# First block's merge-gate and branch projections with tokens on the partitions, and block sums in its down stage for three of eleven pairs

## The chip, the cores and the metric

One core of one Trainium2 chip. The metric is the device time in microseconds of one execution. The kernel before takes 1254.74 us (median of 3 runs, 1254.57 to 1254.82). The core's engines run side by side, each in its own order: TensorE (PE; its weight loads are shown as PEld), VectorE (DVE), ScalarE (ACT), GpSimd (POOL), and SyncE (SP), which issues the loads. They wait for one another by semaphores.

## The reference, cut to what matters

Two transformer blocks on x of 256 tokens by 1024, fp32. The first block's part around the change:

```python
h = rms_norm(x, norm_mix_w)
proj = h @ w_in            # q, kv, gates, q_ret, k_ret, v_ret, g_ret, g_merge (2 * 1024)
y_a = nsa_attention(...) @ w_nsa_branch            # 512 -> 1024
o_r = head_group_norm(retention(...)) * silu(g_ret)
y_b = o_r @ w_ret_branch                           # 1024 -> 1024
gate_a, gate_b = split(sigmoid(g_merge), 2)
x = x + (gate_a * y_a + gate_b * y_b) @ w_mix_out
h = rms_norm(x, norm_ffn_w)
u = causal_dwconv(h @ w_ffn_up)                    # 1024 -> 2 * 2816, width 3
x = x + (silu(u_gate) * u_val) @ w_ffn_down        # 2816 -> 1024
```

The second block has two layers with attention, a convolution and a Fourier branch, a gated merge and the same kind of feed-forward; the change leaves its arithmetic alone.

## The kernel before, in words

**Products.** Every fp32 product is three matmuls with operands split into an upper and a lower part: upper by upper, upper by lower, lower by upper (`mul3`). There are two forms. In `rows` the tokens are stationary (128 of them, half `tt`) and 512 weight columns move (lines 529 to 531): the result has tokens on the partitions. In `feats` 128 weight columns are stationary and all 256 tokens move (lines 584 to 586): the result has features on the partitions. The up stage of the feed-forward has its own form, `wide_feats` (line 608, upper and lower parts of the tokens side by side as 512 columns, then line 613, 256 columns).

**Weights.** `PLAN` lists chunks of 128x2048 (1 MB) in the order of use; `UNITS` names the chunks of each projection. SP loads chunk i into one of six raw buffers when chunk i - 6 has been used (line 436). ACT makes the upper part `whi` (line 1235, four buffers). The lower part `wlo` overwrites the raw chunk; DVE makes it (line 1955), or POOL in four quarters (line 1785) for the chunks in `POOL_LO`, among them three of every four units of the first block's up stage (`POOL_UP`). `splits(last)` makes the parts up to a chunk of the plan; ACT and DVE call it with a chunk three ahead of PE (AHEAD = 3).

**Order.** Each engine's program is written out by hand in the same order of units. `weave(front, back, n)` takes a step of `front` (the attention's small products) and then n steps of `back` (projections that don't depend on it), and runs the rest of `back` at the end. In the first block the back of the attention is vr0, vr1, sg0, sg1 (rows) and three of the eight merge-gate units gm0 to gm7 (feats); the other five stand behind retention. Then follow ya0, ya1 (feats), the transposes of the retention's result, yb0 to yb3 (feats), mo0 and mo1 (`to_x`), the norm n1, the up stage up0_0 to up0_21 and the down stage dn0. The gm units are scaled per token while they leave the banks; as tokens lie along the free axis there, the scale is turned first: two DVE copies (line 2162), two PE transposes (line 703), an ACT copy, and a wait of SP for it (line 133) before it loads tables into the place the scratch had. The merged product is `mg`, features on the partitions, which is what mo needs as stationary operand.

**Up stage.** For unit f ACT copies a bank (`us`, line 1570), makes `whi` of a later chunk, the silu (`fs`), the upper part `ghi` of an earlier product (line 1283) and the convolution's bias term (`fu`, line 1561). DVE does the convolution (line 2469), the product `fg` (line 2492) and the scaling (lines 2479, 2483). POOL makes its weight splits and the lower part `glo` of unit f - 6 (line 1816). `fg` has four buffers.

**Down stage.** Eleven pairs of `g` chunks, 24 matmuls of 512 columns each, into four banks (token half by column half). In the second block's two layers the pairs `SEVEN` = (1, 3, 5, 7), counted from 0, use block sums in the manner of Strassen and Winograd: seven products of blocks in place of eight, 21 matmuls in place of 24. They need a further chunk of sums of weight blocks (`weight_sums`, DVE, lines 1933, 1937, 1939, from the raw chunk, then split like any other), sums of the product's blocks (`g_sums`, POOL, lines 1885 and 1896, with ACT's upper part in between), and at the end `sevens_added` on DVE (line 2533), which adds the kept products to x. The last two or three chunks are ordered so that the first token half ends early: its x add (line 2428) and norm run beside the second half, and PE turns the normed half (line 548).

## Time and profile before

| | |
|---|---|
| median of 3 runs | 1254.74 us (1254.57 to 1254.82) |
| profiled execution | 1254.49 us |
| its span | 1253.2 us |
| instructions | 19361 |
| PE busy | 1247.4 us (100%), 7794 matmuls |
| DVE, ACT, POOL busy | 951.5 (76%), 714.7 (57%), 437.3 us (35%) |
| granted TensorE clock | full in all slices |
| chain that ended last | PE 96% |

A line of the page or of the trace gives an engine, the line of the kernel, the operation, the output and inputs, the shape and the count. Busy time is what the engine executes; a matmul's duration overlaps the next, so the price of a matmul is read from one start to the next. Idle time stands in brackets with what ended it.

### The profile page before, as it was taken

What the parts mean: (1) busy time and instruction counts of PE and PEld (TensorE: products, weight loads), DVE (VectorE), ACT (ScalarE), POOL (GpSimd) and SP (SyncE); (2) the same over time, 40 slices, a digit from 0 to 9 for tenths busy, and PEclk for the clock granted to TensorE, in tenths of its full rate; (3) what the DMA queues carried; (4) which work ended last, traced back from release to release, by engine and by line L of the source; (5) the groups of instructions that cost most, each with busy time, mean ns of one, the idle gap of its engine ahead of it and who ended that gap; (6) DMA issues with size and microseconds to landing.
All of it is one profiled execution on the core that took longest, in us unless ns stands there. A gap on an engine that the chain in (4) does not pass through costs nothing.

```text
span 1253.2 us, 19361 instructions
## 1 busy us (share of the span) xinstructions
PE 1247.4 (100%) x7794; PEld 1120.3 (89%) x7794; DVE 951.5 (76%) x1372; ACT 714.7 (57%) x1026; POOL 437.3 (35%) x346
## 2 busy tenths in 40 slices
PE   9999999999999999999999999999999999999999
PEld 7888899988888889899998888888999998888887
DVE  6865677767887378985767888986898586888895
ACT  7755445377665365575836555545456674655552
POOL 0010011039992069467450112008756743011100
PEclk9999999999999999999999999999999999999999
DMA  7853334545455447644455554555853444545442
GB/s 303 310 211 135 124 129 141 196 185 202 174 197 199 170 168 237 220 164 136 168 191 185 182 200 145 190 210 189 271 188 144 158 168 168 191 181 200 151 166 121
DMA packets 36568, 230.77 MB, mean 184 GB/s; under 512 B 4480, under 2 KB 5120, under 8 KB 10496
## 3 DMA queue, kind: packets, MB, share of 16 engines
q1 hardware_dynamic: 36480, 229.55, 50.9%
q8 instruction: 61, 1.00, 0.3%
q14 instruction: 27, 0.22, 0.1%
HBM read 222.19 MB, written 1.05 MB: 178 GB/s over the span
## 4 chain that ended last, share of the span: by engine, by line
PE 96%; DVE 1%; DMA 1%; ACT 0%; issue 0%; SPq 0%; DVEq 0%
PE ps L608 19%; PE ps L529 10%; PE ps L531 10%; PE ps L530 10%; PE ps L613 10%; PE ps L584 9%; PE ps L585 9%; PE ps L586 9%; PE ps L534 6%; PE ps L548 2%; DMA raw<-in_w 1%; PE ps L677 1%; PE ps L1150 1%; DVE wlo L1955 1%; PE ps L845 0%
## 5 line engine op out<-in xcount | busy, mean ns | idle before, releaser
L1235 ACT ACTIVATE whi<-raw 128x2048 fp32r<-128x2048 f32 (+1 forms) x213 | 401.8, 1891 | 112.6 <-PE ps L531 66.9
L1955 DVE TENSOR_TENSOR wlo<-raw,whi 128x2048 fp32r<-128x2048 f32 (+2 forms) x169 | 383.7, 2276 | 89.0 <-ACT whi L1235 88.0
L1785 POOL TENSOR_TENSOR wlo<-raw,whi 128x512 fp32r<-128x512 f32 x176 | 227.2, 1324 | 90.5 <-ACT whi L1235 87.5
L608 PE MATMUL ps<-hh,whi 128*128 128x512 f32 x1056 | 255.8, 392 | 0.0
L608 PEld LDWEIGHTS ps<-hh,whi 128*128 128x128 f32 x1056 | 193.0, 188 | 36.5
L584 PE MATMUL ps<-hh,whi 128*128 128x256 f32 x640 | 184.1, 288 | 0.0
L586 PE MATMUL ps<-hh,wlo 128*128 128x256 f32 x640 | 181.0, 283 | 0.0
L585 PE MATMUL ps<-hh,whi 128*128 128x256 f32 x640 | 180.9, 283 | 0.0
L1757 POOL TENSOR_TENSOR st<-st,sm 128x1 f32<-128x1 f32 (+2 forms) x28 | 44.8, 1599 | 365.1 <-DVE st L2019 195.1
L613 PEld LDWEIGHTS ps<-hh,wlo 128*128 128x128 f32 x1056 | 137.8, 191 | 6.7
L613 PE MATMUL ps<-hh,wlo 128*128 128x256 f32 x1056 | 139.8, 282 | 0.0
L584 PEld LDWEIGHTS ps<-hh,whi 128*128 128x128 f32 x640 | 122.5, 191 | 0.4 <-issue 0.2
L585 PEld LDWEIGHTS ps<-hh,whi 128*128 128x128 f32 x640 | 122.5, 191 | 0.4 <-issue 0.2
L586 PEld LDWEIGHTS ps<-hh,wlo 128*128 128x128 f32 x640 | 122.4, 191 | 0.0
L2612 DVE SCALAR_TENSOR_TENSOR ps<-gp,sm,ps 128x256 f32<-128x256 f32 x232 | 99.3, 482 | 0.0
L529 PE MATMUL ps<-whi,hh 128*128 128x512 f32 (+1 forms) x248 | 97.9, 395 | 0.0
L531 PE MATMUL ps<-whi,hh 128*128 128x512 f32 (+1 forms) x248 | 95.3, 384 | 0.0
L530 PE MATMUL ps<-wlo,hh 128*128 128x512 f32 (+1 forms) x248 | 95.1, 383 | 0.0
L529 PE MATMUL ps<-whi,ghi 128*128 128x512 f32 x224 | 87.4, 390 | 0.0
L530 PE MATMUL ps<-wlo,ghi 128*128 128x512 f32 x224 | 87.2, 389 | 0.0
L531 PE MATMUL ps<-whi,glo 128*128 128x512 f32 x224 | 87.2, 389 | 0.0
L1570 ACT ACTIVATE fu<-ps 128x512 f32<-128x512 f32 x44 | 26.4, 599 | 101.5 <-PE ps L613 101.5
(350 smaller groups left out, 2266.2 us busy)
## 6 DMA issues: line engine op xcount, KB each, us to landing
raw<-in_w SPq DMA_DIRECT2D x203, 1024.0 KB, 4.8
raw<-in_w SPq DMA_DIRECT2D x8, 256.0 KB, 6.8
kst<-kh SPq DMA_DIRECT2D x16, 128.0 KB, 3.0
qst<-qh SPq DMA_DIRECT2D x16, 128.0 KB, 2.4
raw<-in_w SPq DMA_DIRECT2D x2, 560.0 KB, 12.9
x<-in_x SPq DMA_DIRECT2D x2, 512.0 KB, 5.3
gain<-in_rows SPq DMA_DIRECT2D x2, 512.0 KB, 7.8
kst<-kl SPq DMA_DIRECT2D x8, 128.0 KB, 2.7
```

The costliest lines, as they stand in the source:

```text
L529: pe.op.matmul(o, sh, mh, start=start, stop=False, skip_group_check=True)
L530: pe.op.matmul(o, sh, ml, start=False, stop=False, skip_group_check=True)
L531: signalled(pe.op.matmul(o, sl, mh, start=False, stop=stop, skip_group_check=True), names)
L584: pe.op.matmul(o, wh[:, k, c:c + 128], hi[:, k, :], start=first, stop=False, skip_group_check=True)
L585: pe.op.matmul(o, wh[:, k, c:c + 128], lo[:, k, :], start=False, stop=False, skip_group_check=True)
L586: ins = pe.op.matmul(o, wl[:, k, c:c + 128], hi[:, k, :], start=False, stop=last, skip_group_check=True)
L608: pe.op.matmul(o[:, :], wh[:, k, c], t.hh[:, k, :, :], start=k == 0, stop=False, skip_group_check=True)
L613: ins = pe.op.matmul(o[:, 0:S], wl[:, k, c], t.hhi[:, k, :], start=False, stop=k == 7, skip_group_check=True)
L1235: act.op.activation(t.whi[i % NHI][:, c], t.raw[i % NRAW][:, c], ACT.Copy).then_inc(*at("act_hi", ("hi", i)))
L1785: pool.op.tensor_tensor(t.wlo[i % NRAW][:, half(k)], t.raw[i % NRAW][:, half(k)], t.whi[i % NHI][:, half(k)].bitcast(F32), ALU.subtract).t ...
L1955: dve.op.tensor_tensor(t.wlo[i % NRAW][:, c], t.raw[i % NRAW][:, c], t.whi[i % NHI][:, c].bitcast(F32), ALU.subtract).then_inc(*at("dve_lo ...
L2612: ins = dve.op.scalar_tensor_tensor(t.cv[:, f, :] if j == 30 else acc, t.gp[:, f, j:j + S], cw[:, f, j:j + 1], acc, ALU.mult, ALU.add)
```

## The change

Part A: the merge gates are four units of 512 columns with tokens on the partitions (`rows`) in place of eight with features there; ACT and DVE scale one token half each on the way out of the banks. ya is done by a new form `short_rows`, yb by `rows`. The transposed scale and all that made it are gone. The merged product has tokens on the partitions now and is turned by 16 PE transposes (`mixed_turned`), the first half of the columns inside yb1, the second inside mo. `weave` no longer runs the back out, and the count of back steps behind each front step is given by `behind` and the yields. The x sum of mo takes its chunks in another order. Part B: the plan's down stage is made by one function for all three layers, and the first block's dn0 gets block sums for pairs 3, 5 and 7. POOL makes the differences for pair c, and their lower part, behind glo of unit 2c + 1, between its weight splits; ACT makes the upper part in out(2c + 5) before the bias; DVE's product of unit 2c + 4 waits for the differences; ACT's splits reach one chunk further before the last unit.

```diff
+    def down(unit, name, layer):
+        units[unit] = []
+        for c in range(NFT // 2):
+            units[unit].append(len(plan))
+            plan.append((name, layer, cols((512, 512), (0, 512)) if c in SEVEN[int(unit[2])] else cols((0, 1024)), 2 * c, 2))
+            if c in SEVEN[int(unit[2])]:
+                plan.append((None, layer, range(1024), 2 * c, 2))
...
-    for f in range(8):
-        wide(f"gm{f}", "w_in", 0, cols((4376 + 256 * f, 256)), 8, 8)
+    for n in range(4):
+        in1(f"gm{n}", 4376 + 512 * n, 512)
     for f in range(2):
         wide(f"ya{f}", "w_nsa_branch", 0, cols((512 * f, 512)), 4, 4)
-    for f in range(4):
-        wide(f"yb{f}", "w_ret_branch", 0, cols((256 * f, 256)), 8, 8)
+    for f in range(2):
+        wide(f"yb{f}", "w_ret_branch", 0, cols((512 * f, 512)), 8, 4)
...
-SEVEN = (1, 3, 5, 7)
+SEVEN = (3, 5, 7), (1, 3, 5, 7), (1, 3, 5, 7)
...
-def weave(front, back, n):
+def weave(front, back, n=1):
...
-    run(back)
...
+def behind(tt, place):
+    if place < 3:
+        return (2, (3, 1, 1)[place])[tt]
+    return (2, int(place < 13))[tt]
...
-            sp.wait_ge(*on("rsT", "n0"))
...
-    for tt in range(2):
-        pe.wait_ge(*on("rs wide", "n0", tt))
-    b = fixed_bank(("rsT", "n0"), 5)
-    for tt in range(2):
-        ins = pe.op.transpose(t.ps[b][:, tok(tt)], t.xn[0][:, tok(tt)], ident)
-    ins.then_inc(*at("pe_turned", ("rsT", "n0")))
...
-    back = chain(*[rows(u, *h) for u in ("vr0", "vr1", "sg0", "sg1")], *[feats(f"gm{f}", *h, 8) for f in range(3)])
-    weave(nsa(), back, 2)
+    back = chain(*[rows(u, *h) for u in ("vr0", "vr1", "sg0", "sg1", *(f"gm{n}" for n in range(4)))])
+    weave(nsa(), back)
...
-    weave(retention(), chain(*[feats(f"gm{f}", *h, 8) for f in range(3, 8)]), 3)
-    for f in range(2):
-        run(feats(f"ya{f}", t.oah, t.oal, 4, lambda k: [("free", ("oaT", tt, 0)) for tt in range(2)]))
-        if f == 0:
-            for tt in range(2):
-                for g in range(2):
-                    turned(("orT", tt, g), [("orr gated", tt)], t.orr[tt][:, half(g)], 4, 4 + 2 * tt + g)
-    for f in range(4):
-        run(feats(f"yb{f}", t.orh, t.orl, 8, lambda k: [("free", ("orT", tt, k // 4)) for tt in range(2)]))
+            yield 1
+    weave(retention(), back)
+    run(back)
+    def mixed_turned(f, tt):
+        turned(("mixT", f, tt), [("merged", "mo", f, tt)], t.mg[0][:, tt, half(f)], 4, 4 + 2 * tt + f)
+    for tt in range(2):
+        pe.wait_ge(*on("free", ("oaT", tt, 0)))
+    short_rows("ya0", t.oah, t.oal)
+    for tt in range(2):
+        for g in range(2):
+            turned(("orT", tt, g), [("orr gated", tt)], t.orr[tt][:, half(g)], 4, 4 + 2 * tt + g)
+    short_rows("ya1", t.oah, t.oal)
+    for tt in range(2):
+        for g in range(2):
+            pe.wait_ge(*on("free", ("orT", tt, g)))
+    run(rows("yb0", t.orh, t.orl))
+    g = rows("yb1", t.orh, t.orl)
+    steps(g, 3)
+    for tt in range(2):
+        mixed_turned(0, tt)
+    run(g)
...
+        def mixed(kg, tt):
+            return ("mixed", u, kg // 2 * 2) if m else ("free", ("mixT", kg // 4, tt))
+        part, _, _ = part_of(sum_units(u), t.mh[m], t.ml[m], mixed)
+        if m:
+            for k in range(4):
+                for tt in range(2):
+                    part(0, [k], tt)
+        else:
             for tt in range(2):
-                part(0, [k], tt)
+                part(0, range(4), tt)
+                mixed_turned(1, tt)
...
-            if n and c in SEVEN:
+            if c in SEVEN[n]:
...
+        def sums_upper(f):
+            c = f // 2
+            if f % 2 == 0 and c in SEVEN[n]:
+                upper(("g sums hi", n, c), t.gsh[SEVEN[n].index(c)][:, :, :], t.gs[:, :, :], ("g sums", n, c, "whole"))
         def out(f):
             if f == 0:
...
                 if f >= 1:
                     g_upper(f - 1)
                 silu(f, "scaled")
-                if f % 2 == 0 and f // 2 - 2 in SEVEN:
-                    c = f // 2 - 2
-                    upper(("g sums hi", n, c), t.gsh[SEVEN.index(c)][:, :, :], t.gs[:, :, :], ("g sums", n, c, "whole"))
+                sums_upper(f - 4)
                 return
             if f >= 1:
                 silu(f - 1, "fu")
             if f >= 2:
                 g_upper(f - 2)
+            sums_upper(f - 5)
...
+    def gates_out(n):
+        after = [("kr", "rot", tt) for tt in range(2)] if n == 0 else [("pv", 15)]
+        return value_out(f"gm{n}", lambda tt: t.gm[n][:, tt, :], after, first_scale)
...
-        splits(chunks[0] + AHEAD)
+        splits(chunks[0] + AHEAD + (n == 0))
...
+    def g_sums(n, c):
+        k0, k1 = (t.fg[(2 * c + k) % 4] for k in range(2))
+        a11, a21, a12, a22 = k0[:, 0:128], k0[:, 128:256], k1[:, 0:128], k1[:, 128:256]
+        s3, s5, s6, s7 = (t.gs[:, j, :] for j in range(4))
+        def less(dst, a, b, names=()):
+            pool.op.tensor_tensor(dst, a, b, ALU.subtract).then_inc(*at("pool_small", *names))
+        pool.wait_ge(*on("fg", n, 2 * c + 1))
+        pool.wait_ge(*ev.mine("pool_small"))
+        less(s5, a21, a22)
+        less(s7, a11, a21)
+        pool.wait_ge(*ev.mine("pool_small"))
+        less(s6, a11, s5)
+        pool.wait_ge(*ev.mine("pool_small"))
+        less(s3, a12, s6, [("g sums", n, c, "whole")])
+        pool.wait_ge(*on("g sums hi", n, c))
+        pool.op.tensor_tensor(t.gsl[SEVEN[n].index(c)][:, :, :], t.gs[:, :, :],
+                              t.gsh[SEVEN[n].index(c)][:, :, :].bitcast(F32), ALU.subtract).then_inc(
+            *at("pool_small", ("g sums", n, c)))
     for f in range(NFT + 6):
         if f in POOL_UP:
             split(*UNITS[f"up0_{f}"])
...
             pool.wait_ge(*on("g hi", 0, f - 6))
             pool.op.tensor_tensor(t.glo[:, f - 6, :], t.fg[(f - 6) % 4][:, :], t.ghi[:, f - 6, :].bitcast(F32),
                                   ALU.subtract).then_inc(*at("pool_small", ("g", 0, f - 6)))
+            if f % 2 and (f - 7) // 2 in SEVEN[0]:
+                g_sums(0, (f - 7) // 2)
...
     def ya_out(f):
-        def out(p):
-            j = 4 * f + 2 * p
-            name = (f"ya{f}", p)
+        splits(UNITS[f"ya{f}"][0] + AHEAD)
+        dve.wait_ge(*on("gm sigmoid", f))
+        for tt in range(2):
+            name = (f"ya{f}", tt)
             dve.wait_ge(*on("got", *name))
-            dve.wait_ge(*on("gm sigmoid", f))
-            dve.op.tensor_tensor(t.mg[0][:, j:j + 2, :], pair(name), t.gm[j // 2], ALU.mult).then_inc(
-                *at("dve_out", ("ya gated", j // 2), ("free", name)))
-        return out
+            dve.op.tensor_tensor(t.mg[0][:, tt, half(f)], bank(name)[:, :], t.gm[f][:, tt, :], ALU.mult).then_inc(
+                *at("dve_out", ("free", name)))
+    def first_mixed_lower(f):
+        for tt in range(2):
+            lower([("free", ("mixT", f, tt))], t.ml[0][:, 4 * f:4 * f + 4, tok(tt)],
+                  bank(("mixT", f, tt))[:, :].rearrange("p (k s) -> p k s", k=4),
+                  t.mh[0][:, 4 * f:4 * f + 4, tok(tt)], ("mixed hi", "mo", f, tt))
     def mixed_lower(u, j, m):
         jj = slice(j, j + 2)
...
               ("mixed hi", u, j))
     def yb_out(f):
-        def out(p):
-            name = (f"yb{f}", 0)
+        def out(tt):
+            name, g, m = (f"yb{f}", tt), t.gm[2 + f][:, tt, :], t.mg[0][:, tt, half(f)]
             dve.wait_ge(*on("got", *name))
-            dve.wait_ge(*on("gm sigmoid", 2))
-            dve.op.tensor_tensor(t.gm[4 + f], pair(name), t.gm[4 + f], ALU.mult).then_inc(
-                *at("dve_out", ("free", name)))
-            m = t.mg[0][:, 2 * f:2 * f + 2, :]
+            dve.wait_ge(*on("gm sigmoid", 2 + f))
+            dve.op.tensor_tensor(g, bank(name)[:, :], g, ALU.mult).then_inc(*at("dve_out", ("free", name)))
             await_own("dve_out")
-            dve.op.tensor_tensor(m, m, t.gm[4 + f], ALU.add).then_inc(*at("dve_small", ("merged", "mo", 2 * f)))
-            mixed_lower("mo", 2 * f, 0)
+            dve.op.tensor_tensor(m, m, g, ALU.add).then_inc(*at("dve_small", ("merged", "mo", f, tt)))
...
-                if n and f % 2 == 0 and f // 2 - 2 in SEVEN:
+                if f % 2 == 0 and f // 2 - 2 in SEVEN[n]:
```

## Rows read from the trace of the kernel before

**Rows 1.** The page: busy time, busy tenths of POOL, granted clock, the chain.
```profile
PE 1247.4 (100%) x7794; PEld 1120.3 (89%) x7794; DVE 951.5 (76%) x1372; ACT 714.7 (57%) x1026; POOL 437.3 (35%) x346
...
POOL 0010011039992069467450112008756743011100
PEclk9999999999999999999999999999999999999999
...
PE 96%; DVE 1%; DMA 1%; ACT 0%; issue 0%; SPq 0%; DVEq 0%
```

**Rows 2.** PE's timeline: start us, us, engine, line, operation, out<-in, shape, count.
```profile
220.10 0.28 PE L586 MATMUL ps<-orh,wlo 128*128 128x256 f32 x1
...
238.10 0.28 PE L586 MATMUL ps<-orh,wlo 128*128 128x256 f32 x1
...
386.93 0.40 PE L529 MATMUL ps<-whi,ghi 128*128 128x512 f32 x1
...
445.44 1.03 PE L548 MATMUL ps<-sm,xn 128*128 128x128 f32 x8
```

**Rows 3.** PE's timeline: a piece of twelve, the first after eight transposes, a unit's L613.
```profile
112.27 0.47 PE L529 MATMUL ps<-whi,hh 128*128 128x512 f32 x1
...
115.13 0.38 PE L845 MATMUL ps<-sm,Ex 128*128 128x128 f32 x2
...
446.23 0.47 PE L529 MATMUL ps<-whi,ghi 128*128 128x512 f32 x1
...
373.88 0.40 PE L613 MATMUL ps<-hh,wlo 128*128 128x256 f32 x2
```

**Rows 4.** The waits, queue of SP: waited for, us in total, times, longest.
```profile
SPq L133 <- PE ps L703: 10.8, 1, 10.8
```

**Rows 5.** POOL's timeline in the first block's up stage.
```profile
322.88 5.25 POOL L1785 TENSOR_TENSOR wlo<-raw,whi 128x512 fp32r<-128x512 f32 x4 [1.75 <-ACT whi L1235]
328.08 0.74 POOL L1816 TENSOR_TENSOR glo<-fg,ghi 128x256 fp32r<-128x256 f32 x1
...
339.90 3.50 POOL L1816 TENSOR_TENSOR glo<-fg,ghi 128x256 fp32r<-128x256 f32 x2
...
373.51 2.58 POOL L1816 TENSOR_TENSOR glo<-fg,ghi 128x256 fp32r<-128x256 f32 x1 [0.16 <-ACT ghi L1283]
```

**Rows 6.** POOL's timeline in the second block: one pair's block sums.
```profile
696.89 0.57 POOL L1885 TENSOR_TENSOR gs<-fg,fg 128x128 f32<-128x128 f32 x1 [21.91 <-DVE fg L2492]
...
697.96 1.01 POOL L1885 TENSOR_TENSOR gs<-fg,gs 128x128 f32<-128x128 f32 x2
711.98 2.33 POOL L1896 TENSOR_TENSOR gsl<-gs,gsh 128x512 fp32r<-128x512 f32 x1 [13.02 <-ACT gsh L1283]
```

**Rows 7.** ACT's timeline in the first block's up stage, at unit 11.
```profile
331.46 0.60 ACT L1570 ACTIVATE us<-ps 128x512 f32<-128x512 f32 x1 [1.64 <-PE ps L613]
...
334.06 0.41 ACT L1283 ACTIVATE ghi<-fg 128x256 fp32r<-128x256 f32 x1
334.37 1.01 ACT L1561 ACTIVATE fu<-ps,sm 128x256 f32<-128x256 f32 x2
```

**Rows 8.** DVE's timeline: a unit of the first up stage, and weight sums.
```profile
380.97 1.77 DVE L2469 SCALAR_TENSOR_TENSOR fu<-ps,sm,fu 128x255 f32<-128x255 f32 x4
...
384.33 2.28 DVE L1955 TENSOR_TENSOR wlo<-raw,whi 128x2048 fp32r<-128x2048 f32 x1
...
797.83 1.22 DVE L1933 TENSOR_TENSOR raw<-raw 128x1024 f32<-128x1024 f32 x1
...
799.81 0.69 DVE L1939 TENSOR_TENSOR raw<-raw,raw 128x512 f32<-128x512 f32 x1
```

**Rows 9.** DVE's timeline: kept sums of dn1, and the x add of dn0.
```profile
834.43 0.69 DVE L2533 TENSOR_TENSOR x<-x,dsum 128x512 f32<-128x512 f32 x1
...
839.72 2.29 DVE L1955 TENSOR_TENSOR wlo<-raw,whi 128x2048 fp32r<-128x2048 f32 x1
...
438.15 0.69 DVE L2428 TENSOR_TENSOR x<-ps,x 128x512 f32<-128x512 f32 x1 [3.11 <-PE ps L531]
```

More of the change, by code:

```diff
@@ L1446, in nsa @@
     def nsa():
-        yield
+        yield 2
         n = 0
         for tt in range(2):
-            for _ in compressed(tt):
-                yield
+            compressed(tt)
+            for place in range(3):
+                yield behind(tt, place)
                 n += 1
@@ L1476, in act_program @@
         rows("sg1", value_out("sg1", lambda tt: t.sg[:, tt, 512:1024], kr_read, first_scale)),
-        *[feats(f"gm{f}", 8) for f in range(2)],
+        *[rows(f"gm{n}", gates_out(n)) for n in range(4)],
     )
-    weave(nsa(), back, 2)
-    splits(UNITS["gm2"][0] + AHEAD)
+    weave(nsa(), back)
     heads_upper("oaT", 4, t.oah)
@@ L1490, in retention @@
                 act.op.activation(t.sg[:, :, :], t.sg[:, :, :], ACT.Silu).then_inc(*at("act_small", ("sg silu",)))
-            yield
-    weave(retention(), chain(*[feats(f"gm{f}", 8) for f in range(3, 8)]), 3)
-    act.wait_ge(*on("free", ("gm7", 0)))
+            yield 2 - n % 2
+    weave(retention(), back)
+    run(back)
+    act.wait_ge(*ev.mine("act_out"))
     def gates_sigmoid(n):
-        g = t.gm_all[n]
+        g = t.gm[n][:, :, :]
+        act.wait_ge(*on("free", (f"gm{n}", 0)))
         act.op.activation(g, g, ACT.Sigmoid).then_inc(*at("act_small", ("gm sigmoid", n)))
@@ L1526, in to_x @@
         norm_squares(norm, 1, (), (1,))
-    to_x("mo", "n1", [("free", ("yb3", 0))])
+    to_x("mo", "n1", [("free", ("yb1", tt)) for tt in range(2)])
     fc = small(t, "fconv").rearrange("p (f v c) -> p f v c", f=NFT, v=2)
```

146 lines of the change are left out of this document (62 added, 84 removed).

## The prediction

> **What bounds the kernel now.** I read the page first: TensorE (PE) is busy for 1247.4 of 1253.2 us, the granted clock is full in all 40 slices (the 2.4 GHz level), and the chain that ended last is 96% PE [rows 1]. So every PE slot taken away shortens the run by itself, until some other engine is late for PE; and the places that can make it late are those where another engine has no spare time. POOL's digits name one: 3, 9, 9, 9, 2 in the slices from 251 to 407 us, where the first block's up stage runs; only two slices elsewhere reach 8 or 9 [rows 1]. Then I read PE's timeline for the pitch, start to next start, of each shape, and the timelines of POOL, ACT and DVE in the stretch where the second part of the change puts its work. The profiled execution took 1254.49 us, 1.29 more than its span; the median shown is 1254.74, 0.25 above it. I sum against 1254.49 and add the 0.25 at the end. About 0.2% (2.5 us) is what a measurement of this kernel can tell from no change.
>
> **PE's prices.** With weights stationary and 256 tokens moving, 150 matmuls lie between the two L586 rows: 18.00/150 = 0.120 us each. With tokens stationary and 512 weight columns moving, the down stage's 258 matmuls from 386.93 to 445.44 give 58.51/258 = 0.227 [rows 2]. Two of the first do the work of one of the second: 0.240 against 0.227, a gain of 0.013 for a pair. After a break (attention's small products between) a piece costs more: twelve 512-column ones took 115.13 - 112.27 = 2.86 instead of 2.72, +0.14. For pieces of 256 columns I take half of that. Eight transposes take 446.23 - 445.44 = 0.79 [rows 2, 3], with the break behind them 0.92; four are half of the 0.79 and 0.1, 0.50.
>
> The Trainium skill (TensorE: Matmul & The Clock Gate, "Back-to-back issue gap") gives an isolated gap of N/2.4 + 2.5 ns, that is 215.8 ns for 512 columns and 109.2 for 256; by that a pair would save 2.5 ns, and the 336 pairs below 0.8 us in place of 4.3, so that the first part would cost 2.6 us more than I sum. The same section's sustained figure for 512 columns, 131 ns, is not what this trace shows. The trace has 227 and 120 ns, and these go into the sum.
>
> **Part A, projections with tokens on the partitions.**
> - gm: 384 matmuls of 256 become 192 of 512: 46.1 to 43.6 us. Before, some 17 pieces each pay a break of 0.07 (1.2); after, 16 pieces of 12 pay 0.13 to 0.14 (2.2) [rows 2, 3]. Net -1.5.
> - ya: 96 become 48, 11.52 to 10.90: -0.6. yb: 192 become 96, 23.04 to 21.79: -1.2 [rows 2].
> - The merged product has to be turned: 16 new transposes, as a group of 8 in yb1 and two groups of 4 in mo: 0.9 + 2 x 0.50 = +1.9 [rows 2, 3].
> - The transposed norm scale goes: two transposes, with their break 0.3 by the same rows (0.2 and 0.1); two small DVE copies and one ACT copy; and SP's wait for it, 10.8 us long [rows 4]. SP's next issues (the decay tables, then weights) move earlier only; nothing on PE waited for them: 0.
> - Vector work: the gates' scaling is 8 DVE products of 128x512 before, and is 4 on DVE and 4 on ACT after. DVE stands idle 24% and ACT 43% of the span [rows 1], and these engines' spare time stands around these products: 0. The merged product is split per 512 columns behind its transposes. A late split would show at mo; with 0.9 us of transposes and nine yb1 steps in between I count 0, at most 0.5.
> Sum of A: -1.5 - 0.6 - 1.2 + 1.9 - 0.3 = -1.7, between -2.4 (the new breaks cost 0.1 each) and -0.3 (a late split of 0.5, and transposes at half as much again).
>
> **Part B, block sums for pairs 3, 5, 7 (counted from 0) of dn0.** PE does 21 products in place of 24: 9 x 0.227 = -2.0 [rows 2]. No DMA is added: the sum chunk is made in SBUF from the raw one. What it adds stands elsewhere:
> - POOL, in the up stage. It has, for each four units of 5.57 (22.3 us), three weight splits of 5.25, and glo at 0.74, 0.74 and 3.50 for two; it shows one pause, of 1.75 us, in front of the first [rows 5]. The change adds for each pair 2.1 us of differences and a lower part between 1.27 (a quarter split, 5.25/4) and 2.33 [rows 5, 6]: 3.4 at the least for 1.75 of pause. I take 1.27, since the split is of the same shape, 128x512, in the same stretch; 2.33 is for rival 3.
> - That lower part waits, in POOL's own order, for ACT's upper part. After g(7) (328.08, ends 328.8) the differences end at 330.9; ACT comes to that place behind its ghi of 334.06 [rows 5, 7], so the upper part ends at 335.0, the lower at 336.2. The split of unit 14, behind it, starts 7.4 us after its 328.8. PE wants it only at 373.88 - 5 x 5.57 = 346.0 [rows 3] (the unit of 5.57 is half of 386.93 - 373.88 less the 1.91 of one L613 group), so this one is covered.
> - Pair 5: POOL is 7.4 late less its pause; its differences end at 359.2, while ACT stands there at 334.06 + 22.27 + 0.31 = 356.6. Now ACT waits 2.6, in front of the bias of unit 15, and DVE's convolution behind it. POOL's split of 18 starts 361.1, of 19 at 369.2 and ends at 374.5; PE wants it at 373.9 [rows 3], and a release takes some 0.1: PE waits 0.5.
> - Pair 7: the split of 21 ends 383.5 (two DVE splits of 2.28 that POOL can't work beside push it back), g(15) and the differences end 388.3; ACT would be there at 382.6 and waits 5.7. Behind it all is one chain: upper part (0.6) and bias (0.9 from start to start, as 334.37 has it) to 389.8 [rows 7]; convolution, product and scaling take 384.33 - 380.97 = 3.4 a unit and DVE's split 2.2 [rows 8]. So unit 19's and the split are done at 395.6, unit 20's at 399.0, the first weight sums (1.2 + 0.7 + 0.7) at 401.7 [rows 8]. Then ACT makes the upper part of the chunk of sums (1.9), and bias and convolution of unit 21 and two products follow to 407.6; DVE's lower part of the sums (2.2) ends at 409.8. PE, at 0.5 late and three pairs of 5.44 into dn0, wants this chunk after nine of pair 3's 21 products, at 386.9 + 0.5 + 16.3 + 2.0 = 405.9 (0.2 for breaks) [rows 2]: PE waits 3.9.
> - The end of dn0. DVE adds the kept sums, 834.43 to 839.72, and has one more split (2.3) in front of the x add [rows 9]; it comes to them some 1.3 us later here, with the order of splits the same. In dn0 the x add then starts 2.6 us after its product is ready, in place of at once (438.15). From that add to PE's transposes at 445.44 the norm's chain takes 7.3 us and had 1.65 us to spare at its first half and 0.3 at the second (an estimate from its two halves' lengths, 0.75 and 1.8 at the last step): PE waits 1.4 to 2.3. I take 2.3, since POOL's and DVE's splits collide there.
> - DVE and ACT in dn0 gain three sum chunks (2.7 + 2.2 and 1.9 each); a pair of 5.44 has one split of 2.28 in dn0, so some 3 us of DVE are free in each: 0 beyond the chain above.
> Sum of B: -2.0 + 0.5 + 3.9 + 2.3 = +4.7. Lengths of one instruction varied by 2% move it between 3.6 and 5.9.
>
> The shared cause is that POOL and DVE do not work on two SBUF operands at once: glo takes 0.74 alone and 2.58 in the stretch where DVE's wlo runs [rows 5]. The Trainium skill (GPSIMD Engine Reference, "1. Specifications") says that the two share their SBUF interface for such instructions; the trace agrees.
>
> **Forecast.** 1254.49 - 1.7 + 4.7 = 1257.5, plus 0.25: 1257.7 us.
>
> **Rivals.**
> 1. *Not slower: POOL keeps up.* The three weight splits ahead of PE are slack: unit 14's comes 7.4 late and is still 4.7 early. If the differences cost less beside DVE than I take, or ACT's upper part falls into its idle 1.64 us before each unit [rows 7], POOL's lateness does not add up from pair to pair, and pair 7's chain ends before 405.9. That decides: the last lower part of pair 3's sums before or after 405.9. Left are -2.0 and the end's 1.4: B = -0.6, A -1.7: 1252.4. For it: the slack. Against it: 3.4 us for 1.75 of pause, three times.
> 2. *Half of it.* ACT's wait at pair 7 comes out at 3 us in place of 5.7 and PE's 3.9 falls to about 1: 1254.8.
> 3. *More.* If the lower part takes 2.33 as in the second block [rows 6] and each difference stretches beside DVE as glo does (x3.5 at worst), POOL is some 3 to 8 us later by pair 7, and PE waits at units 18, 19 and 21 too: 1261 to 1264.
> 4. *Part A doesn't pay*: breaks or a late mixT split eat the 1.7; added to the forecast it is 1259.4.
>
> **How the numbers follow.** Forecast case 0.42 (its own range 1255.5 to 1260), rival 1 0.28, rival 2 0.12, rival 3 0.12, rival 4 0.06. Range for 8 in 10: from the middle of rival 1, with A at its best, 1251.7, to 1260.2 (leaves out most of rival 3 and the lower tail of rival 1). Faster by over 0.2% (below 1252.2): the better half of rival 1 and a little, 0.18. Within: the rest of rival 1, rival 2, and the forecast case below 1257.2 (some 0.14): 0.39. Slower: 0.43.
>
> **What would show it.** Right: PE's idle time in the span from 5.8 us (1253.2 - 1247.4) to about 12; a PE wait of 3 to 5 us in pair 3 of dn0 with DVE's wlo as what ended it; ACT's waits for gs growing (0, 2.6, 5.7) over the three pairs; POOL full from 328 to 391; the span of yb at 0.227 a matmul; PE waiting for xn at the end of dn0. Wrong: no PE wait between 370 and 412 (rival 1); POOL's L1785 rows unshifted after 336; a gm stretch not shorter than before (rival 4). If PE's idle time stays near 5.8 and the time still isn't below 1252, my pitches are at fault and not the coupling.

## The result and the profile after

The kernel after takes 1256.73 us (median of 17 runs, 1256.49 to 1258.28) against 1254.57 for the kernel before in the same series (17 runs, 1253.73 to 1255.45): 2.2 us slower by the medians. The ratio is 1.0020, with a 95% interval of [1.0014, 1.0026]. The forecast was 1257.7 with 1251.7 to 1260.2. The profiled execution took 1257.91 us, 1.2 above its median; the start of the experiments says what is known of that.

The page of the kernel after, the lines that answer to [rows 1]:

```profile
span 1256.3 us, 18745 instructions
...
PE 1246.7 (99%) x7463; PEld 1104.5 (88%) x7463; DVE 969.4 (77%) x1386; ACT 723.8 (58%) x1037; POOL 449.0 (36%) x361
...
PE 89%; POOL 5%; DVE 2%; issue 1%; ACT 1%; DMA 1%; SPq 0%; POOLq 0%; DVEq 0%; ACTq 0%
```

PE has less work, its share of the last chain fell from 96% to 89%, and POOL and DVE came into it. The timeline of PE in the first block's up and down stages of the kernel after shows where it waits (the bracket is the idle time and what ended it):

```profile
372.84 2.17 PE L628 MATMUL ps<-hh,wlo 128*128 128x256 f32 x16 [0.34 <-POOL wlo L1831]
...
389.34 0.50 PE L534 MATMUL ps<-whi,ghi 128*128 128x512 f32 x1 [1.81 <-DVE fu L2510]
...
447.08 0.63 PE L553 MATMUL ps<-sm,xn 128*128 128x128 f32 x4 [0.54 <-DVE xn L2068]
448.75 0.63 PE L553 MATMUL ps<-sm,xn 128*128 128x128 f32 x4 [1.04 <-DVE xn L2068]
```

None of these waits was there before. POOL's timeline in the kernel after, to compare with [rows 5]:

```profile
326.55 0.74 POOL L1885 TENSOR_TENSOR glo<-fg,ghi 128x256 fp32r<-128x256 f32 x1
327.43 0.47 POOL L1865 TENSOR_TENSOR gs<-fg,fg 128x128 f32<-128x128 f32 x1
327.86 0.46 POOL L1865 TENSOR_TENSOR gs<-fg 128x128 f32<-128x128 f32 x1
328.40 1.01 POOL L1865 TENSOR_TENSOR gs<-fg,gs 128x128 f32<-128x128 f32 x2
333.53 1.29 POOL L1876 TENSOR_TENSOR gsl<-gs,gsh 128x512 fp32r<-128x512 f32 x1 [4.13 <-ACT gsh L1311]
334.78 5.25 POOL L1831 TENSOR_TENSOR wlo<-raw,whi 128x512 fp32r<-128x512 f32 x4
...
374.33 7.30 POOL L1831 TENSOR_TENSOR wlo<-raw,whi 128x512 fp32r<-128x512 f32 x4
381.59 0.74 POOL L1885 TENSOR_TENSOR glo<-fg,ghi 128x256 fp32r<-128x256 f32 x1
382.47 2.32 POOL L1865 TENSOR_TENSOR gs<-fg,fg 128x128 f32<-128x128 f32 x1
```

At pair 3 POOL stands 4.13 us idle for ACT's upper part. The next split, which started right behind glo in the kernel before (at 328.78, where glo ends), starts at 334.78, 7.5 us behind the end of glo. The differences of pair 7 it makes from 382.5 to 386.3; dn0 begins at 385.98. ACT's timeline in the kernel after shows what that does to ACT:

```profile
357.64 0.63 ACT L1311 ACTIVATE gsh<-gs 128x512 fp32r<-128x512 f32 x1 [2.44 <-POOL gs L1865]
...
386.32 0.63 ACT L1311 ACTIVATE gsh<-gs 128x512 fp32r<-128x512 f32 x1 [5.40 <-POOL gs L1865]
386.86 1.00 ACT L1606 ACTIVATE fu<-ps,sm 128x256 f32<-128x256 f32 x2
```

and DVE's what it does to DVE:

```profile
387.90 1.78 DVE L2510 SCALAR_TENSOR_TENSOR fu<-ps,sm,fu 128x255 f32<-128x255 f32 x4 [3.42 <-ACT fu L1606]
```

ACT waits 0, 2.44 and 5.40 us at the three pairs (forecast 0, 2.6, 5.7). The convolution of unit 19 ends its reading of that unit's two banks late, and dn0's third group of matmuls, which takes one of them (bank 6), waits for it: that is the 1.81 us at 389.34. Behind it comes a thing I had not expected, in the windows of the kernel after (the stretch, its length, PE busy, then weight loads, DVE, ACT, POOL, the granted clock, DMA share, GB/s):

```profile
385.00:390.00 5.00, 3.19 (x19) 2.51 (x18) 2.07 (x6) 3.68 (x5) 3.79 (x6) 1.00 0.53 193
390.00:395.00 5.00, 5.00 (x17) 3.91 (x16) 4.93 (x8) 3.64 (x7) 0.73 (x1) 0.66 0.04 16
395.00:400.00 5.00, 5.00 (x24) 4.13 (x23) 4.86 (x9) 0.31 (x1) 0.00 (x0) 1.00 0.58 210
```

From 390 to 395 the granted clock is 0.66 in the mean: eight matmuls of 512 columns stand 0.43 us apart in place of 0.227, the 1.2 GHz level. They take 1.6 us more than at 2.4 GHz.

### The profile page after: what moved, and what is told of

Same layout as the page of the kernel before. It is cut to its first block, busy times and chain, and to the rows that moved or that the text cites. A ratio compares the mean times of both kernels' runs of the same rounds, so it can differ in the third digit from the quotient of the medians.

```text
span 1256.3 us, 18745 instructions
## 1 busy us (share of the span) xinstructions
PE 1246.7 (99%) x7463; PEld 1104.5 (88%) x7463; DVE 969.4 (77%) x1386; ACT 723.8 (58%) x1037; POOL 449.0 (36%) x361
## 4 chain that ended last, share of the span: by engine, by line
PE 89%; POOL 5%; DVE 2%; issue 1%; ACT 1%; DMA 1%; SPq 0%; POOLq 0%; DVEq 0%; ACTq 0%
PE ps L623 16%; PE ps L534 12%; PE ps L536 12%; PE ps L535 12%; PE ps L628 8%; PE ps L589 7%; PE ps L591 7%; PE ps L590 7%; PE ps L539 6%; POOL wlo L1831 3%; PE ps L553 2%; DMA raw<-in_w 1%; POOL glo L1885 1%; DVE wlo L2003 1%; POOL gs L1865 1%
## 5 line engine op out<-in xcount | busy, mean ns | idle before, releaser
L2003 DVE TENSOR_TENSOR wlo<-raw,whi 128x2048 fp32r<-128x2048 f32 (+2 forms) x172 | 390.8, 2279 | 67.9 <-ACT whi L1263 67.0
L623 PEld LDWEIGHTS ps<-hh,whi 128*128 128x128 f32 x1056 | 193.0, 188 | 36.4
L589 PE MATMUL ps<-hh,whi 128*128 128x256 f32 x512 | 146.1, 285 | 0.0
L591 PE MATMUL ps<-hh,wlo 128*128 128x256 f32 x512 | 144.9, 283 | 0.0
L590 PE MATMUL ps<-hh,whi 128*128 128x256 f32 x512 | 144.8, 283 | 0.0
L628 PEld LDWEIGHTS ps<-hh,wlo 128*128 128x128 f32 x1056 | 137.7, 191 | 7.4 <-POOL wlo L1831 0.8
L628 PE MATMUL ps<-hh,wlo 128*128 128x256 f32 x1056 | 139.9, 283 | 0.3 <-POOL wlo L1831 0.3
L534 PE MATMUL ps<-whi,hh 128*128 128x512 f32 (+1 forms) x312 | 125.0, 401 | 0.5 <-DVE wlo L2003 0.5
L536 PE MATMUL ps<-whi,hh 128*128 128x512 f32 (+1 forms) x312 | 120.5, 386 | 0.0
L535 PE MATMUL ps<-wlo,hh 128*128 128x512 f32 (+1 forms) x312 | 120.1, 385 | 0.0
L590 PEld LDWEIGHTS ps<-hh,whi 128*128 128x128 f32 x512 | 98.0, 191 | 0.1
L591 PEld LDWEIGHTS ps<-hh,wlo 128*128 128x128 f32 x512 | 98.0, 191 | 0.0
L589 PEld LDWEIGHTS ps<-hh,whi 128*128 128x128 f32 x512 | 97.9, 191 | 0.1
L534 PE MATMUL ps<-whi,ghi 128*128 128x512 f32 x209 | 82.4, 394 | 1.8 <-DVE fu L2510 1.8
L535 PE MATMUL ps<-wlo,ghi 128*128 128x512 f32 x209 | 82.0, 393 | 0.0
L536 PE MATMUL ps<-whi,glo 128*128 128x512 f32 x209 | 81.9, 392 | 0.0
```

The costliest lines, as they stand in the source:

```text
L534: pe.op.matmul(o, sh, mh, start=start, stop=False, skip_group_check=True)
L535: pe.op.matmul(o, sh, ml, start=False, stop=False, skip_group_check=True)
L536: signalled(pe.op.matmul(o, sl, mh, start=False, stop=stop, skip_group_check=True), names)
L589: pe.op.matmul(o, wh[:, k, c:c + 128], hi[:, k, :], start=first, stop=False, skip_group_check=True)
L590: pe.op.matmul(o, wh[:, k, c:c + 128], lo[:, k, :], start=False, stop=False, skip_group_check=True)
L591: ins = pe.op.matmul(o, wl[:, k, c:c + 128], hi[:, k, :], start=False, stop=last, skip_group_check=True)
```

## The experiments

**How they are compared.** The time up to PE's first product of the attention (`k1h`) differs from execution to execution: 90.28 us in the profile of the kernel after, 88.7 to 90.4 in those below, 89.83 in that of before. It holds the first loads, which no experiment touches. It also holds the two transposes of the scale, at 32 us, which Part A removes (the kernel before has 537 matmuls in this stretch, those with Part A 535). The profiled time of the kernel after, 1257.91 less 90.28, is 1167.63, and that of repeat_first below (1256.42 less 88.82) 1167.60, although the first execution is 1.5 us longer: the 1.5 us lie in this first stretch. That the profile of the kernel after lies 1.2 above its median is not shown to come from there, since the other executions have no profile. So beside the timed ratio I give three stretches of the profiled execution, read from PE's starts: S1, from that product to the first of dn0; S2, from there to the second block's first product (`hh` as moving or stationary operand); S3, the rest to the last matmul.

```
                   S1      S2      S3     sum      ratio to before, 95%
before           297.09   60.77  802.41  1160.27
after            295.70   64.61  802.63  1162.94   1.0020 [1.0014, 1.0026]
a_alone          295.15   60.76  802.47  1158.38   0.9983 [0.9974, 0.9992]
b_alone          297.82   64.59  802.63  1165.04   1.0038 [1.0025, 1.0051]
lower_later      295.13   60.24  802.64  1158.01   0.9984 [0.9975, 0.9993]
upper_behind_b.  296.55   62.80  802.61  1161.96   1.0019 [1.0010, 1.0028]
repeat_first     295.70   64.61  802.56  1162.87   1.0028 [1.0016, 1.0039]
pairs_35         295.70   59.63  802.40  1157.73   0.9980 [0.9971, 0.9988]
lower_twice      295.14   63.31  802.58  1161.03   1.0007 [0.9998, 1.0016]
split_behind     295.70   64.84  802.15  1162.69   1.0029 [1.0018, 1.0040]
q7_later         295.11   58.96  802.58  1156.65   0.9970 [0.9961, 0.9980]
all_four         295.12   67.52  802.52  1165.16   1.0031 [1.0019, 1.0042]
turns_twice      297.44   64.62  802.61  1164.67   1.0031 [1.0019, 1.0042]
```

### Each part alone

a_alone, the kernel after without the block sums in dn0:

```diff
-SEVEN = (3, 5, 7), (1, 3, 5, 7), (1, 3, 5, 7)
+SEVEN = (), (1, 3, 5, 7), (1, 3, 5, 7)
...
-        splits(chunks[0] + AHEAD + (n == 0))
+        splits(chunks[0] + AHEAD)
...
```

> Part A alone: the kernel after with no block sums in dn0 (and ACT's splits back to three ahead). Theory (A pays, B's coupling costs): 1.9 us faster than the kernel before, 1252.5 to 1253.0; in the trace PE's idle time returns to about that of before, no clock below full, gm about 2.0 us shorter, ya 0.6, yb with its eight transposes 0.35, mo 1.1 longer. Rival (A does not pay, its transposes and breaks eat the gain): within 0.5 of the kernel before, 1254.1 to 1255.1.

b_alone is the kernel before with the block sums alone: `down`, `SEVEN`, `sums_upper`, `g_sums` and DVE's wait as in the diff of the change, nothing of its other half.

> Part B alone: the kernel before with block sums for pairs 3, 5, 7 of dn0, the orders of POOL, ACT and DVE as in the kernel after. Theory: it is B that costs: 3.5 to 4.5 us slower than before where the clock falls behind the PE wait, 2 to 3 where it does not, so 1256.6 to 1259; PE waits 1.5 to 2.5 us at the third bank of dn0's first pair. Rival (A and B disturb each other, each alone is harmless): within 1 us of before.

Measured: A 1252.1 us against 1254.3 of before, ratio 0.9983, a little better than I expected; B 1258.92, ratio 1.0038, as expected. The product of the two, 1.0021, is the ratio of the whole change. In the stretches A takes 1.94 us off S1 and leaves S2 alone; B adds 0.73 to S1 (0.5 of it the wait at unit 19; the other 0.2 I can't place) and 3.82 to S2. The stretches of the whole change are the sums of the two to within 0.2 us (S1 -1.39 for -1.94 and +0.73, S2 +3.84 for -0.01 and +3.82), so the two parts do not disturb each other by more. B's PE waits, from PE's timeline in b_alone:

```profile
374.28 2.18 PE L616 MATMUL ps<-hh,wlo 128*128 128x256 f32 x16 [0.34 <-POOL wlo L1792]
...
390.76 0.50 PE L532 MATMUL ps<-whi,ghi 128*128 128x512 f32 x1 [1.78 <-DVE fu L2478]
...
409.54 0.50 PE L532 MATMUL ps<-whi,gsh 128*128 128x512 f32 x1 [1.46 <-DVE wlo L1964]
```

Here a second wait of 1.46 us stands at pair 3's sums, which the kernel after did not have, and the clock stays at 1.00 behind the first. This second wait is the one that the prediction had named. S2 is 64.59, the kernel after's 64.61.

### Is it the wait or the clock, and what sets the stretch?

repeat_first gives PE work where it would wait for the bank:

```diff
                 for tt in range(2):
+                    if n == 0 and (c, k, tt) == (0, 0, 1):
...
+                        for hf in (0, 1, 0):
+                            mul3(t.ps[banks[0, hf]][:, :], t.ghi[:, 0, tok(0)], t.glo[:, 0, tok(0)], wh[:, 0, half(hf)],
+                                 wl[:, 0, half(hf)], True, False)
```

> The kernel after, with nine matmuls repeated on PE in dn0 just where it would wait for the bank (three groups of the first pair, started anew, the same result): 2.04 us of PE work in place of 1.96 of idle time. Theory (the stretch to pair 3's sums chunk is set by DVE's chain; a wait or a slower clock before it only shifts where PE's time goes): from the first matmul of dn0 to the last before the turned norm 60.0 to 60.5 us as in the kernel after (60.17) and in part B alone (60.18), the clock stays full, a wait of 1.4 to 1.8 us stands at the sums of pair 3, 1256.4 to 1257. Rival (the fall of the clock behind the idle time costs its 1.6 us): that stretch 58.5 to 59, 1255 to 1255.6 if most executions had the fall.

Measured: S2 64.61, to the last digit that of the kernel after; the clock full; PE's timeline in repeat_first has one wait in dn0 ahead of the norm:

```profile
406.64 0.50 PE L534 MATMUL ps<-whi,gsh 128*128 128x512 f32 x1 [1.49 <-DVE wlo L2009]
```

The stretch is set by DVE's chain to the lower part of the sums chunk. What PE does before it, idle, slow or doing work twice, only moves time from one place to another; the clock's 1.6 us in the kernel after stand where otherwise this wait would. They fill it to the last tenth, which is luck: by the same sum a longer fall of the clock would have cost time. The timed runs agree that the fall costs nothing. The mean granted clock is on record as 0.999 for 8 of the 17 executions of the kernel after, the profiled one among them, and as 1.000 for 9; their medians are 1256.67 and 1256.79 us. The median of this kernel, 1257.71, lay above the 1257 I expected while its profile (1256.42) lay at the lower end; the stretches give no reason, and it stays open. Its ratio, 1.0028 [1.0016, 1.0039], can't be told from that of the kernel after.

### POOL's order

lower_later takes the waiting instruction one unit further down POOL's list:

```diff
         less(s3, a12, s6, [("g sums", n, c, "whole")])
+        if n:
+            g_sums_lower(n, c)
+
+    def g_sums_lower(n, c):
         pool.wait_ge(*on("g sums hi", n, c))
...
                 g_sums(0, (f - 7) // 2)
+            if f % 2 == 0 and (f - 8) // 2 in SEVEN[0]:
+                g_sums_lower(0, (f - 8) // 2)
```

> The kernel after with one move on POOL: the lower part of each pair's sums (which waits for ACT's upper part) stands one unit later, behind the next weight split and glo. The same work on every engine. Theory (POOL's wait of 4.1 us at pair 3 and the lateness it starts is the cause): POOL idles less than 0.5 there, ACT waits less than 1 us at pair 7 in place of 5.4, PE has no wait over 0.3 us between 365 and 410 and the clock stays full; A's -1.9, the nine matmuls' -2.0 and the end's +2.0 are left: 1252.4 to 1253.2. Rival (the added work itself, 3.4 us of POOL a pair and DVE's 8 us of weight sums, is too much in any order): PE still waits 1.5 us or more near 387 or 405, 1255 to 1256.7.

Measured: 1252.19 us, ratio 0.9984, 0.2 under what I expected and 4.5 us less than the kernel after (4.3 when each is set against the kernel before in its own series); S2 60.24. POOL's timeline in lower_later:

```profile
326.85 1.01 POOL L1865 TENSOR_TENSOR gs<-fg,gs 128x128 f32<-128x128 f32 x2
327.81 5.24 POOL L1831 TENSOR_TENSOR wlo<-raw,whi 128x512 fp32r<-128x512 f32 x4
333.00 0.76 POOL L1889 TENSOR_TENSOR glo<-fg,ghi 128x256 fp32r<-128x256 f32 x1
333.69 1.31 POOL L1880 TENSOR_TENSOR gsl<-gs,gsh 128x512 fp32r<-128x512 f32 x1
```

and ACT's at pair 7:

```profile
378.11 0.63 ACT L1311 ACTIVATE gsh<-gs 128x512 fp32r<-128x512 f32 x1 [0.44 <-POOL gs L1865]
```

The same instructions, no idle time on POOL from 319.8 to 382.8, 0.44 us of wait on ACT in place of 5.40, no PE wait between 365 and 410. Of the change's loss in S2 all but the end is gone.

lower_twice is that kernel with each lower part computed twice on POOL.

```diff
         pool.wait_ge(*on("g sums hi", n, c))
+        if n == 0:
+            pool.op.tensor_tensor(t.gsl[SEVEN[n].index(c)][:, :, :], t.gs[:, :, :],
+                                  t.gsh[SEVEN[n].index(c)][:, :, :].bitcast(F32), ALU.subtract).then_inc(
+                *at("pool_small"))
+            pool.wait_ge(*ev.mine("pool_small"))
```

> The kernel with POOL's lower parts one unit later, and POOL makes each of the three lower parts twice (the same values): 1.3 us or more of work a pair added, 4 to 6 us over the three, where the kernel after had 4.1 us of waiting at pair 3. Theory (it is lateness of POOL at pair 7 that costs, whether from a wait or from work, and some 2 us of it are free): ACT waits 3 to 4 us at pair 7, PE waits 0.5 to 2 us between unit 19 and the sums of pair 3, so 1252.7 to 1254.5. Rival (a wait in POOL's order costs, work does not): within 0.4 us of the kernel with single lower parts, from the first matmul of the up stage to the next layer's first.

Measured: 1255.45 us; S2 63.31, 3.1 us more than lower_later. ACT's wait at pair 7 is longer than I expected, and PE's first wait short:

```profile
384.35 0.63 ACT L1311 ACTIVATE gsh<-gs 128x512 fp32r<-128x512 f32 x1 [6.84 <-POOL gs L1865]
```

```profile
387.38 0.50 PE L534 MATMUL ps<-whi,ghi 128*128 128x512 f32 x1 [0.50 <-DVE fu L2521]
```

The second wait, at pair 3's sums, is 1.46. So it is not waiting as such that costs: work in the same place costs too. What counts is how late POOL has the differences of pair 7, and not how long ACT waits for them: ACT waits longer here than in the kernel after (6.84 against 5.40), and the kernel is faster. ACT's upper part of pair 7 starts 0.33 us after dn0's first matmul in the kernel after and 0.97 before it here, and pair 3's sums start on PE 22.12 and 20.81 us after dn0's first matmul: 21.8 us lie between the two in both, and as many in b_alone, repeat_first, split_behind and turns_twice. In lower_later the upper part starts 5.73 before dn0. The chain would then be ready at 16.1, and PE gets there at 18.39 without a wait: POOL has some 2.3 us to spare.

My numbers for this run were too low (ACT 3 to 4 us, 1252.7 to 1254.5). POOL had the differences of pair 7 ready 4.8 us later than in lower_later. Two second lower parts stand ahead of them and account for 2.8, and the first lower part of pair 5, which now fell beside a DVE split, took 3.34 us in place of 1.48.

pairs_35 leaves pair 7 out (`SEVEN[0] = (3, 5)`).

> The kernel after with block sums in dn0 for pairs 3 and 5 alone: three matmuls more, no sums for pair 7. Theory (POOL's lateness adds up and only pair 7 turns it into a PE wait; the end is late since the kept sums are added right in front of the x add): no PE wait over 0.6 us from 365 to 410 but the one at unit 19, none for xn at the end over 0.3; A's -2.2 (as measured alone), -1.36 for six matmuls, +0.3: 1250.8 to 1251.6. Rival (each pair costs alike): a third less than the kernel after loses, 1254.5 to 1256.

Measured: 1251.61 us (expected up to 1251.6), S1 295.70 with the wait at unit 19 as in the kernel after, S2 59.63, which is 60.77 less six matmuls (1.36) and 0.2. Without pair 7 dn0 loses nothing: the waits in the middle are gone, and so are those at the end, where the kept sums now come two pairs earlier. Pair 7 without 3 and 5 I did not run, so what it costs by itself isn't shown; it stands on the lateness that the others leave.

### ACT's order

upper_behind_bias moves `sums_upper(f - 5)` behind the bias in `out(f)`.

> The kernel after with one step moved on ACT: the upper part of a pair's sums stands behind the bias of that unit, no longer in front of it. Theory (ACT's wait of 5.4 us for POOL at pair 7 holds the bias of unit 19, and by that DVE's convolution 19 and the bank that PE's third group of dn0 needs): the bank is free in time, the PE wait of 1.96 us near 387 falls under 0.5, and the chain to the lower part of the sums chunk is shorter by about the bias and the convolution, 1.0 to 2.6 us: 1254.0 to 1255.8. Rival (the order on ACT does not matter, POOL's or DVE's own work sets both places): 1256.3 to 1257.

Measured: 1256.67 us, outside of what my theory had (1254.0 to 1255.8); the ratio, 1.0019, can't be told from that of the kernel after, though the sum of the stretches is 1.0 us shorter. Half of the theory holds: the wait for the bank is gone and S2 is 1.8 us shorter. But S1 is 0.85 longer. PE's timeline in upper_behind_bias:

```profile
366.58 2.17 PE L628 MATMUL ps<-hh,wlo 128*128 128x256 f32 x16 [0.86 <-POOL wlo L1831]
...
405.93 0.50 PE L534 MATMUL ps<-whi,gsh 128*128 128x512 f32 x1 [1.76 <-DVE wlo L2003]
```

With ACT's upper part 0.9 us later at pairs 3 and 5, POOL, which waits for it, is that much later with the splits behind it, and unit 18's is now late as well. The time is the rival's, its reason (that ACT's order does not matter) is not. I had looked at the order of one of two engines that wait for each other.

### The end of dn0

split_behind moves the DVE split that stood in front of the x add behind the first half's x adds and gains:

```diff
                 sevens_added(n)
+                if n == 0:
+                    break
 
         down_added(n, after, 0)
+        if n == 0:
+            splits(chunks[-3] + AHEAD)
```

> The kernel after with one move on DVE at the end of dn0: the split of the next projection's first chunk, which stood between the kept sums and the x add, stands behind the x adds and gains of the first token half. Theory (the x add is late because of that split): PE's two waits for xn (0.54 and 1.04 us) fall to 0.3 or less in sum plus the order of turning, 1.3 to 1.9 us faster than the kernel after, 1254.9 to 1255.5. Rival (the norm's own chain through ACT and POOL sets the end, or the moved split makes the next projection wait): less than 0.4 us gained, 1256.3 to 1256.8.

Measured: 1257.88 us, no gain and above both expectations; ratio 1.0029, S2 0.2 longer, S3 0.5 shorter. DVE's timeline in split_behind:

```profile
438.18 0.69 DVE L2469 TENSOR_TENSOR x<-ps,x 128x512 f32<-128x512 f32 x1
...
440.85 2.28 DVE L2003 TENSOR_TENSOR wlo<-raw,whi 128x2048 fp32r<-128x2048 f32 x1
...
444.38 3.46 DVE L2068 SCALAR_TENSOR_TENSOR xn<-xn,st,gain 128x512 f32<-128x512 f32 x2 [0.81 <-POOL st L1803]
```

and POOL's:

```profile
444.32 5.92 POOL L1831 TENSOR_TENSOR wlo<-raw,whi 128x512 fp32r<-128x512 f32 x4
```

Counted from dn0's first matmul the x add starts 2.1 us earlier (53.2 in place of 55.3), but the moved split fills DVE's pause before the norm's mean, so that the scaling of xn starts only 0.8 earlier. And POOL's split, by now ready, starts with it: the two instructions of the scaling take 3.46 us in place of 2.42. The theory's cause was right and the cure was wrong.

q7_later moves two additions that only the second token half needs, on top of lower_later:

```diff
-        dve.wait_ge(*on("got", f"dnP{n}", 3))
-        added(x(1, 0), q7, x(1, 0))
...
-        added(x(1, 1), x(1, 1), q7, ALU.subtract, [("free", (f"dnP{n}", 3))])
...
             norm_scaled(after, 0)
+            if n == 0:
+                last_product()
             norm_lower(after, 0)
```

(`last_product` makes the two additions; in the second block they stay in their place.)

> The kernel with POOL's lower parts one unit later (1252.2 measured), with one further move on DVE: the two additions of the seventh product, to the second token half, stand behind the norm's scaling of the first half, in place of in front of the x add. Theory (the x add is 1.8 us late, DVE busy with the kept sums): the x add and the norm 1.4 us earlier, PE's waits for xn (0.24 and 1.05) fall to 0.4 or less in sum: 1251.0 to 1251.5. Rival (POOL's weight split, which DVE's scaling of xn cannot run beside, sets the second wait whatever the x add does): the first wait goes, the second stays near 1: 1251.9 to 1252.2.

Measured: 1250.69 us, 0.3 under what I expected, ratio 0.9970 [0.9961, 0.9980], S2 58.96. PE turns both halves of the normed tokens with no wait:

```profile
440.48 1.24 PE L553 MATMUL ps<-sm,xn 128*128 128x128 f32 x8
```

S2 is now 60.77 (that of before) less 2.04 for the nine matmuls, plus 0.23. This version beats both kernels, the kernel before by 3.6 us.

all_four adds pair 1 to it (`SEVEN[0] = (1, 3, 5, 7)`).

> The best kernel so far (lower parts one unit later, seventh product's additions later, 1250.7) with pair 1 of dn0 by block sums too. Three matmuls less: -0.68. Theory (the room at the end of the up stage is what limits: the weight sums of pair 1 fall on DVE, 2.7 us of sums and 2.2 of a further split, while the units 20 and 21 are still to be convolved, and a further 3.4 us fall on POOL): PE waits 2 us or more at the first pairs, 1252 to 1255. Rival (room is left): 1250.0.

Measured: 1258.59 us, above what I expected; S2 is 8.6 us longer than in q7_later, for three matmuls less. PE's timeline in all_four, and a window of it:

```profile
387.50 0.50 PE L534 MATMUL ps<-whi,ghi 128*128 128x512 f32 x1 [0.47 <-DVE fu L2516]
...
393.33 0.47 PE L534 MATMUL ps<-whi,ghi 128*128 128x512 f32 x1 [1.45 <-DVE fu L2516]
...
399.25 0.77 PE L534 MATMUL ps<-whi,gsh 128*128 128x512 f32 x1 [3.61 <-DVE fu L2516]
```

```profile
400.00:405.00 5.00, 5.00 (x14) 3.84 (x13) 4.90 (x5) 1.84 (x3) 2.92 (x2) 0.50 0.00 0
```

The expectation had only a part of the reason. All three waits are ended by a convolution, and none by the weight sums of pair 1, which DVE makes early (378.8 to 382.2). The first wait, for unit 19's bank, is POOL's lateness, as in lower_twice: ACT waits 6.50 us for the differences of pair 7. The other two are for banks as well. The block sums keep four products apart, in banks 0 to 3, and up to the last convolutions these banks hold units 20 and 21. DVE's timelines in all_four, and in q7_later, which has no sums for pair 1:

```profile
391.81 1.77 DVE L2516 SCALAR_TENSOR_TENSOR fu<-ps,sm,fu 128x255 f32<-128x255 f32 x4
...
397.72 1.77 DVE L2516 SCALAR_TENSOR_TENSOR fu<-ps,sm,fu 128x255 f32<-128x255 f32 x4
```

```profile
396.21 1.78 DVE L2516 SCALAR_TENSOR_TENSOR fu<-ps,sm,fu 128x255 f32<-128x255 f32 x4 [1.71 <-ACT fu L1606]
```

Unit 21's convolution, the last of these rows in each kernel, ends 14.0 us after dn0's first matmul in both. In all_four PE wants bank 2, which unit 21 holds, some 10 us after that matmul; in q7_later pair 3 wants it after 16 to 18. So pair 1 comes too early for the banks, and room on POOL and DVE for its sums would not change that. (This is read from the kernels and the traces; no kernel with that convolution moved was run.) Here the clock's fall is not hidden either: 13 matmuls at 0.43 in place of 0.227 add 2.6 us to 5.5 us of waits, and no further wait of PE in dn0 gets shorter by it.

### The price of the transposes

turns_twice makes each group of four transposes of the merged product twice, into the same bank.

> The kernel after with each of the 16 transposes of the merged product made twice in a row. It prices them in place: theory 16 x 0.10 = 1.5 to 1.8 us from the first matmul of the attention (L534 on k1h) to the first of dn0 (295.70 in the kernel after), 1258 to 1259; rival (the transposes stand in PE time that is waiting anyway, for the split of the merged product): less than 0.5 us.

Measured: 1258.35 us and S1 297.44, both as expected: 1.74 us more for 16 transposes. PE's timeline in turns_twice (L935 are the added ones):

```profile
229.06 0.60 PE L935 MATMUL ps<-sm,mg 128*128 128x128 f32 x4
229.50 0.60 PE L553 MATMUL ps<-sm,mg 128*128 128x128 f32 x4
229.93 0.60 PE L935 MATMUL ps<-sm,mg 128*128 128x128 f32 x4
230.37 0.60 PE L553 MATMUL ps<-sm,mg 128*128 128x128 f32 x4
```

They are on the path in full, 0.11 us each.

## Why the prediction was right

The forecast case came in, and its mechanism but for the place of one wait: its own sum was +3.0 (-1.7 and +4.7), the stretches show +2.7 and the medians +2.2. The measured 1256.73 us lies within 0.2% of the kernel before, not above it, so of the three outcomes (faster, within 0.2%, slower) the one came in that was given 0.39, and not the one that was given 0.43. Step by step:

- **A, forecast -1.7.** S1 of a_alone: -1.94. ya went from 13.25 to 12.65 us, -0.60 as forecast. yb with its group of eight transposes went from 23.04 to 22.69, -0.35, as the forecast's -1.2 and +0.9 give. That leaves +1.0 for mo with its two groups, as forecast. gm and the rest of the attention took -1.97 against a forecast of -1.5: this term was 0.5 too small, for a reason that I did not look for. The -0.3 for the turned scale is no part of S1: its two transposes stand at 32 us, where they and the break behind them take 0.2. So in S1 the forecast is -1.4 for the measured -1.94, and that the sum of A comes so near to -1.7 is in part luck. The 16 transposes come to 1.9 us in place (0.90 in yb, 0.96 in mo), as forecast, and to 1.74 by doubling them, which adds no breaks. The vector work I had set at nothing is hidden: a_alone's S1 has no PE wait that before does not have.
- **B, nine matmuls, -2.04.** q7_later's S2 has them all but 0.23.
- **Unit 19, forecast a wait of 0.5.** 0.51 (a pitch of 0.73 in place of 0.227, of which the profile shows 0.34 as idle). The times in the prediction, 374.5 and 0.1 against 373.9, give 0.7 and not the 0.5 that it took. The wait is gone in lower_later, S1 295.13 against 295.70.
- **Pair 7's chain, forecast 3.9.** From dn0's first matmul to the first turn it takes 61.10 us in the kernel after. The kernel before takes 58.51; less 2.04 for the nine matmuls, plus 0.70 for the wait at the first turn, that is 57.17, which leaves 3.9 for the chain. Pair 3's sums were forecast 22.4 us after dn0's first matmul (409.8, less 386.9 and the 0.5 of unit 19) and came after 22.12. The size was right, the place wrong: a PE wait of 3 to 5 us at pair 3 was named as a sign, and the kernel after has no wait there. I had not looked at the banks. dn0's third group takes a bank of unit 19, which the held convolution frees late, and PE waits there first (1.96 by the pitch); the slow clock then took the other 1.6. In b_alone, where the clock stays full, the two waits are 1.78 and 1.46. Both places hang on the one chain, ACT's wait at pair 7, so they share one cost and don't add up; repeat_first shows it.
- **The end of dn0, forecast 2.3 (1.4 to 2.3).** 0.70 before the first turn and 1.25 between it and the second block's first product: 1.95. The x add started 2.2 us after its product was ready in place of 2.6.
- **PE's idle time, forecast about 12.** 1256.3 - 1246.7 = 9.6 us. The fall of the clock turned 1.6 us of wait into slow work, which counts as busy.
- **POOL full from 328 to 391** did not come in as it was written: POOL stood idle for 4.13, 0.74 and 0.74 us in front of the lower parts. The prediction's own sum had the first of these (330.9 to 335.0).
- **The other price of a pair.** At 2.5 ns in place of 13 the sum of A would move by 4.3 less 0.8, 3.5 us, and not by the 2.6 that the prediction says; ya's 0.60 us for 48 pairs is 12.5 ns a pair.
- **Rival 1** (POOL keeps up) is what lower_later is: 1252.2 against 1252.4. It fails in the kernel as written because POOL waits in front of its lower parts, 4.13 us at pair 3 and 0.74 at pair 5; lower_later moves these waits and nothing else. **Rival 3**: the lower part took 1.29, not 2.33, and only one difference of pair 7 was stretched (2.32 in place of 0.5). **Rival 4** is excluded by a_alone.

The medians' 2.2 stands below the stretches' 2.7; the kernel before varied by 1.7 us between executions in the same series, so this difference says nothing.

## What to carry to other kernels

An engine with 1.75 us of pause in 22 can take a little more work, but no wait on top of it: before giving it work, ask where in its list it waits for somebody who runs on another rhythm, and put that step where the answer is already there; here one instruction moved one unit down the list was worth 4.5 us. When one instruction is late, follow everything that its engine holds, banks too, to the first place where the bound engine needs it; several such places on one chain cost once. And at the end of a stage, put what the next stage's first half doesn't need behind the chain that it does need, rather than moving the biggest piece. Before a product is made in another form, see who still holds the banks that this form takes.
